# Low parts written over the raw weights, four buffers for the high parts, and the loads gated by TensorE

## What is computed

```python
proj = h @ w_in             # several, 2048 deep, up to 6680 wide; also w_out, w_kv, w_cq ...
x = x + y @ w_out
scores -> top 16 of 128x128 keys per head -> gate[token, expert]
a = gelu(h @ w_u.T) * gate  # w_u: 16384 x 2048
x = x + a @ w_v             # w_v: 16384 x 2048
```

## Time and profile before

| | us |
|---|---|
| median of 3 runs | 3142.95 |
| the profiled execution | 3144.03 |
| its span (first to last instruction) | 3141.9 |
| TensorE busy | 3003.1 |
| VectorE busy | 1890.5 |
| ScalarE busy | 1363.6 |

### The profile page before, as it was taken

How to read it: one execution, slowest core, us unless ns; L and a number is a source line. 1 busy time by engine, 2 the same in 40 slices (tenths; PEclk the granted TensorE clock), 3 DMA queues, 4 the chain that set the end, 5 groups by cost and what they waited for, 6 DMA issues and landing times. The chain is left out here.

```text
span 3141.9 us, 41649 instructions
## 1 busy us (share of the span) xinstructions
PE 3003.1 (96%) x16258; PEld 2576.6 (82%) x16258; DVE 1890.5 (60%) x2383; ACT 1363.6 (43%) x1511; POOL 5.3 (0%) x8
## 2 busy tenths in 40 slices
PE   8999978899998999999899999999999999999998
PEld 6878777789877788877899988878888888888887
DVE  4546775555676544565568988855555445554445
ACT  4543454444444343345434444433344344434344
POOL 0000000000000000000000000000000000000000
PEclk9999999899999999999999999999999999999999
DMA  6554435145442555444345455565655655545553
GB/s 249 187 189 175 175 129 175 59 163 188 161 169 103 178 184 183 165 155 161 129 156 184 164 186 206 203 234 187 241 187 187 241 196 188 189 175 194 207 191 143
DMA packets 94113, 560.54 MB, mean 178 GB/s; under 512 B 10552, under 2 KB 26544, under 8 KB 31920
## 3 DMA queue, kind: packets, MB, share of 16 engines
q1 hardware_dynamic: 73152, 522.03, 47.1%
q10 hardware_dynamic: 20848, 36.95, 3.1%
HBM read 543.15 MB, written 15.73 MB: 178 GB/s over the span
## 5 line engine op out<-in xcount | busy, mean ns | idle before, releaser
L2052 DVE TENSOR_TENSOR w_lo<-raw,w_hi 128x2048 fp32r<-128x2048 f32 (+2 forms) x500 | 1130.7, 2262 | 1100.7 <-ACT w_hi L1354 1095.8
L1354 ACT ACTIVATE w_hi<-raw 128x2048 fp32r<-128x2048 f32 (+2 forms) x500 | 945.6, 1892 | 1182.8 <-PE ps L767 414.5
L765 PE MATMUL ps<-w_hi,hT 128*128 128x512 f32 (+3 forms) x1344 | 523.6, 390 | 28.9 <-DVE w_lo L2052 28.4
L767 PE MATMUL ps<-w_hi,hT 128*128 128x512 f32 (+3 forms) x1344 | 515.4, 383 | 0.0
L766 PE MATMUL ps<-w_lo,hT 128*128 128x512 f32 (+3 forms) x1344 | 515.1, 383 | 0.0
L1226 PE MATMUL ps<-hT,w_hi 128*128 128x512 f32 x1536 | 486.4, 398 | 1.2 <-DVE x L2982 0.7
L1268 PE MATMUL ps<-w_hi,c_hi 128*128 128x512 f32 x1024 | 401.1, 392 | 11.9 <-DVE c_lo L2942 11.9
L1270 PE MATMUL ps<-w_hi,c_lo 128*128 128x512 f32 x1024 | 399.8, 390 | 0.0
L1269 PE MATMUL ps<-w_lo,c_hi 128*128 128x512 f32 x1024 | 399.8, 390 | 0.0
L1230 PEld LDWEIGHTS ps<-hT,w_lo 128*128 128x128 f32 x1536 | 289.2, 188 | 68.5
L765 PEld LDWEIGHTS ps<-w_hi,hT 128*128 128x128 f32 x1344 | 255.6, 190 | 80.3 <-DVE w_lo L2052 23.5
(11 more groups left out here) (274 smaller groups left out, 3324.6 us busy)
## 6 DMA issues: line engine op xcount, KB each, us to landing
raw<-in_w_u_t SPq DMA_DIRECT2D x128, 1024.0 KB, 4.8
raw<-in_w_v SPq DMA_DIRECT2D x128, 1024.0 KB, 5.2
raw<-in_w_in_2.0 SPq DMA_DIRECT2D x32, 1024.0 KB, 4.7
raw<-in_odd_w.0 SPq DMA_DIRECT2D x20, 1024.0 KB, 4.7
raw<-in_even_w.3608 SPq DMA_DIRECT2D x16, 1024.0 KB, 4.9
raw<-in_w_out.0 SPq DMA_DIRECT2D x16, 1024.0 KB, 4.8
raw<-in_w_out.1 SPq DMA_DIRECT2D x16, 1024.0 KB, 4.8
raw<-in_w_out_2.0 SPq DMA_DIRECT2D x16, 1024.0 KB, 4.8
```

What stands on the lines that cost most here:

```text
L765: pe.matmul(o, hi, wh, start=(j + k == 0), stop=False)
L767: mm = pe.matmul(o, lo, wh, start=False, stop=(j == 3 and k == 3))
L1354: act.activation(w_hi[:, s % 2, 0:size], raw[:, s, 0:size], ACT.Copy).then_inc(hi_done, 1)
L2052: dve.tensor_tensor(w_lo[:, s % 2, 0:size], raw[:, s, 0:size], w_hi[:, s % 2, 0:size].bitcast(F32), ALU.subtract).then_inc(lo_done, 1)
```

## The change

SBUF use stays the same: 64 KB of each partition held four raw buffers and two each for w_hi and w_lo, and now hold four for w_lo and four for w_hi. `raw` is a second name for the memory of `w_lo` (the same address, type float32). DVE now writes the low part of an item over its raw values. Four things follow in the code:

- The load of item n waits until PE has finished item n-4 (`item_used`), where it waited for DVE's split of item n-4.
- ACT's split waits for the landing alone. That the buffers are free follows from the landing, since the load waited for PE.
- PE, ACT and DVE take buffer n % 4 (in unrolled loops `s` or `j`) in place of n % 2.
- In six places (seven waits, since one stands in a program run for both layers) ACT's side work, which read what ACT itself had evacuated, now waits for its own evacuation (`evac_act`).

The order of instructions on every engine is as it was. What has changed is what they wait for; ACT's 24 register instructions that worked out the values of the removed wait in loops are gone too.

```diff
+RAW_AT = 4096 + 4 * (NT * D + KC * 2 * S)
...
-    raw = sb("raw", [P, RAW, 2048])
-    w_hi = sb("w_hi", [P, 2, 2048], F32R)
-    w_lo = sb("w_lo", [P, 2, 2048], F32R)
+    w_lo = sb("w_lo", [P, RAW, 2048], F32R)
+    w_hi = sb("w_hi", [P, RAW, 2048], F32R)
+    raw = nc.alloc_sbuf_tensor_at("raw", [P, RAW, 2048], F32, offset=RAW_AT)
...
             if n >= RAW:
-                sp.wait_ge(lo_done, n - RAW + 1)
+                sp.wait_ge(item_used, n - RAW + 1)
...
                 for s in range(RAW):
-                    sp.wait_ge(lo_done, 4 * i + (base + s - RAW + 1))
+                    sp.wait_ge(item_used, 4 * i + (base + s - RAW + 1))
...
-                            wh = w_hi[:, j % 2, k * width:(k + 1) * width]
-                            wl = w_lo[:, j % 2, k * width:(k + 1) * width]
+                            wh = w_hi[:, j, k * width:(k + 1) * width]
+                            wl = w_lo[:, j, k * width:(k + 1) * width]
...
         def split(q, s, size):
 
-            if not isinstance(q, int) or 4 * q + s >= 2:
-                act.wait_ge(item_used, 4 * q + (s - 1))
             act.wait_ge(landed[s], 16 * q + 16)
-            act.activation(w_hi[:, s % 2, 0:size], raw[:, s, 0:size], ACT.Copy).then_inc(hi_done, 1)
+            act.activation(w_hi[:, s, 0:size], raw[:, s, 0:size], ACT.Copy).then_inc(hi_done, 1)
...
         def memory_side(l):
             loaded()
+            act.wait_ge(evac_act, g_m[l].act0 + 2)
             act.wait_ge(evac_dve, g_m[l].dve0 + 2)
...
             dve.wait_ge(hi_done, 4 * q + (s + 1))
-            dve.tensor_tensor(w_lo[:, s % 2, 0:size], raw[:, s, 0:size], w_hi[:, s % 2, 0:size].bitcast(F32),
+            dve.tensor_tensor(w_lo[:, s, 0:size], raw[:, s, 0:size], w_hi[:, s, 0:size].bitcast(F32),
                               ALU.subtract).then_inc(lo_done, 1)
```

More of the change, by code:

```diff
@@ L821, in out_part @@
                         hi, lo = hT_hi[:, 4 * j + k, t * P:(t + 1) * P], hT_lo[:, 4 * j + k, t * P:(t + 1) * P]
-                        wh, wl = w_hi[:, n % 2, k * COLS:(k + 1) * COLS], w_lo[:, n % 2, k * COLS:(k + 1) * COLS]
+                        wh, wl = w_hi[:, n % RAW, k * COLS:(k + 1) * COLS], w_lo[:, n % RAW, k * COLS:(k + 1) * COLS]
                         pe.matmul(o, hi, wh, start=begins and k == 0, stop=False)
@@ L962, in cmp_gemm @@
                         hi, lo = c_hi[:, q % 2, l * 32:l * 32 + 32], c_lo[:, q % 2, l * 32:l * 32 + 32]
-                        wh = w_hi[:, n % 2, l * CMP_HID:(l + 1) * CMP_HID]
-                        wl = w_lo[:, n % 2, l * CMP_HID:(l + 1) * CMP_HID]
+                        wh = w_hi[:, n % RAW, l * CMP_HID:(l + 1) * CMP_HID]
+                        wl = w_lo[:, n % RAW, l * CMP_HID:(l + 1) * CMP_HID]
                         first, last = q + l == 0, q == 3 and l == 7
@@ L1152, in _ @@
                     hi, lo = hT_hi[:, k, t * P:(t + 1) * P], hT_lo[:, k, t * P:(t + 1) * P]
-                    wh, wl = w_hi[:, n % 2, k * 512:(k + 1) * 512], w_lo[:, n % 2, k * 512:(k + 1) * 512]
+                    wh, wl = w_hi[:, n % RAW, k * 512:(k + 1) * 512], w_lo[:, n % RAW, k * 512:(k + 1) * 512]
                     pe.matmul(o, hi, wh, start=(k == 0), stop=False)
@@ L1201, in _ @@
                         kc = 4 * j + k
-                        pe.matmul(o, w_hi[:, n % 2, a:a + P], hT_hi[:, kc], start=first, stop=False,
+                        pe.matmul(o, w_hi[:, n % RAW, a:a + P], hT_hi[:, kc], start=first, stop=False,
                                   skip_group_check=True)
-                        pe.matmul(o, w_hi[:, n % 2, a:a + P], hT_lo[:, kc], start=False, stop=False,
+                        pe.matmul(o, w_hi[:, n % RAW, a:a + P], hT_lo[:, kc], start=False, stop=False,
                                   skip_group_check=True)
-                        mm = pe.matmul(o, w_lo[:, n % 2, a:a + P], hT_hi[:, kc], start=False, stop=last,
+                        mm = pe.matmul(o, w_lo[:, n % RAW, a:a + P], hT_hi[:, kc], start=False, stop=last,
                                        skip_group_check=True)
@@ L1225, in activations @@
                     for k in (k0, k0 + 1):
-                        pe.matmul(ps[:, s % 2, :], w_hi[:, s % 2, k * P:(k + 1) * P],
+                        pe.matmul(ps[:, s % 2, :], w_hi[:, s, k * P:(k + 1) * P],
                                   hT[:, k].rearrange("p n t -> p (n t)"), start=(k == 0), stop=False,
@@ L1229, in activations @@
                     for k in (k0, k0 + 1):
-                        mm = pe.matmul(ps[:, s % 2, 0:S], w_lo[:, s % 2, k * P:(k + 1) * P], hT_hi[:, k], start=False,
+                        mm = pe.matmul(ps[:, s % 2, 0:S], w_lo[:, s, k * P:(k + 1) * P], hT_hi[:, k], start=False,
                                        stop=(k == KC - 1), skip_group_check=True)
@@ L1236, in activations @@
             for k in range(KC):
-                wh, wl = w_hi[:, s % 2, k * P:(k + 1) * P], w_lo[:, s % 2, k * P:(k + 1) * P]
+                wh, wl = w_hi[:, s, k * P:(k + 1) * P], w_lo[:, s, k * P:(k + 1) * P]
                 pe.matmul(o, wh, hT_hi[:, k], start=(k == 0), stop=False)
@@ L1266, in outputs @@
                 ch, cl = c_hi[:, s % 2, t * P:(t + 1) * P], c_lo[:, s % 2, t * P:(t + 1) * P]
-                wh, wl = w_hi[:, s % 2, n * 512:(n + 1) * 512], w_lo[:, s % 2, n * 512:(n + 1) * 512]
+                wh, wl = w_hi[:, s, n * 512:(n + 1) * 512], w_lo[:, s, n * 512:(n + 1) * 512]
                 pe.matmul(o, ch, wh, start=first and b in fresh, stop=False, skip_group_check=True)
@@ L1521, in keys_side @@
         def keys_side():
+            act.wait_ge(evac_act, g_memkv[1].act0 + 2)
             act.wait_ge(evac_dve, g_memkv[1].dve0 + 2)
@@ L1582, in first_side @@
             yield from st.pair_at(AT_K)
+            act.wait_ge(evac_act, g_akv.act0 + 3)
             act.wait_ge(evac_dve, g_akv.dve0 + 3)
@@ L1590, in first_side @@
             yield from st.until(AT_B_SQUARES)
+            act.wait_ge(evac_act, g_b.act0 + 2)
             act.wait_ge(evac_dve, g_b.dve0 + 2)
@@ L1664, in first_side @@
             yield from st.until(AT_GATES)
+            act.wait_ge(evac_act, g_gz.act0 + 3)
             act.wait_ge(evac_dve, g_gz.dve0 + 3)
@@ L1741, in index_side @@
             yield from st.until(AT_C_SILU)
+            act.wait_ge(evac_act, g_cz.act0 + 3)
             act.wait_ge(evac_dve, g_cz.dve0 + 3)
```

## The result

The changed kernel took **3103.75 us** (median of 4 runs, 3102.60 to 3105.16) against 3142.97 us (4 runs, 3141.54 to 3145.56): ratio 0.9877, 95% interval 0.9865 to 0.9889. It is faster by 39.2 us. I had forecast 20 us, and 3103.75 lies under the range's lower end of 3111. The profiled execution took 3103.42 us, its span is 3101.3 us.

A forecast was written before the change was run, and what follows sets the result against it. TensorE, busy 3003.1 of 3141.9 us, was taken as the bound, so only its waits or clock drops could be won: 22.5 us won less 2.0 lost, 20.5 off 3144.0, about 3123 us for the median; range 3111 to 3137.

The forecast's parts named there:

- the slack: Usual cycle in V: time between a split item being ready and TensorE needing it grows from 1.2 to 6.7 us.
- the four waits named: TensorE's waits of L765 for w_lo at 149, 192, 477 and 928 us would be gone in the changed profile.
- those between 380 and 445 us: TensorE's waits of 4.3 and 1.9 us for w_lo and 13.6 us would stand, ACT and DVE being the limit; gain 0.
- the other edits: Waits on `evac_act`, subtraction over its own input, and four buffers in place of two: taken as costing 0.
- ACT and DVE were not the limit: Rival, chance 0.17: the chain of ACT and DVE takes the waits over; about 3135 us.
- TensorE's waits did not move elsewhere: Rival, chance 0.10: waits were hidden or merely move to attention, turns or barriers; gain within 6 us, 3137 to 3149 us.
- the usual load of V: Rival, chance 0.05, slower: in U and V, landings above 11.9 us put loads on TensorE's path; 3172 us at 12.1 us.
- U0, 3.8 in six: Loop U0: six TensorE waits on w_lo, 3.8 us in all, of which 3.0 us would be won.
- That is what the 18 waits are.: TensorE's waits on w_lo after the start, 30.2 us, come from ACT or DVE side work exceeding 1.2 us of slack.
- 320 to 345 us: Three TensorE waits, 4.3 us: the first two (1.6) go, the third (2.7) follows the last evacuation; 2.5 us won.
- I take one such loss: In V, one weight load near a fetch of gates lands after 13.5 us and costs TensorE 2.0 us.
- all 30.2 us go: Range's lower end: all w_lo waits in question and four clock drops of 1.5 us go, 36 us, 3107; range ended at 3111.

The follow-up runs named there:

- the gate: ACT's split of item n waits until TensorE ends item n-2, which the change removed; put back in every split of the new kernel: 3160.76 us.
- the gate in U0 alone: New kernel with ACT's wait for TensorE's end of item n-2 put back in the 32 splits of loop U0: 3116.60 us.
- the gate put back at three places: New kernel with ACT's wait for the end of item n-2 put back for items 88 to 111, 146 to 153 and 223 to 230: 3112.19 us.
- the two runs with the gate everywhere: New kernel with ACT's wait for the end of item n-2 in every split: 3160.76 us; the same with second and third fetch in pieces: 3150.74 us.
- the version with a lead of one item: New kernel with ACT's split of item n waiting for TensorE's end of item n-3: 3107.78 us.

## Why the prediction was half right

The mechanism was right: the gate made the waits (restored, it brings them back), the slack grew by 5.0 us, to 6.0, the four waits named went away at their places, those between 380 and 445 us stood, the other edits cost nothing, and a load behind a fetch came late. The rivals fell: ACT and DVE were not the limit at the places named, TensorE's waits did not move elsewhere, and the usual load of V takes its 5.3 us. What failed is the price: the prediction took the listed idle time of TensorE's waits on w_lo for the whole cost of the gate, and its range was built on that. The sizes one by one:

- **"U0, 3.8 in six, DVE is nearly full with choosing. I take 3.0."** The gate's part was 8.5, shown by the gate in U0 alone and its companions; another 1.6 us of the 10.1 were a drop of the clock at item 277 that one execution had and the other not, which is luck. I took the listed idle time for the price. A stall costs what lies between the starts, and here 0.66 us for 0.41 listed; eight of 14 stalls were listed nowhere. That DVE was nearly full was no limit: with a lead it was never late.
- **"That is what the 18 waits are."** The list of waits on w_lo is not the list of what the gate costs. 11.7 us were won in stretches for which I had no term (items 83 to 130, 146 to 160, 161 to 245), and the gate put back at three places there cost 6.2 us of it again. One form can be read off the views: ahead of item 150 TensorE waited 2.1 us at the matmuls of L823 for a turned activation, put down to issue. After the change that wait is gone, and with the gate back at items 146 to 153 it returns (the last row of that experiment). The other form is that of U0.
- **320 to 345 us, "I take 2.5"** was 5.1 over items 32 to 60. I had given back the third wait as fixed behind the last evacuation; it shrank from 2.70 to 1.76 us. Another 1.6 us are a drop of the clock at item 53 that the new kernel's profiled run lacks. That is luck too, since the same kernel profiled again has it. Most of the rest is the first two waits.
- **"I take one such loss", 2.0 us** was 8.5 us in two. The formula held: landing + 0.4 - 11.9 gives 2.6 and 4.0 us for landings of 14.1 and 15.5 us, and TensorE's waits are 2.63 and 3.99. The landing was wrong. The row of before that I used (13.5 us) was of a load issued 4.5 us behind its fetch. In the new kernel load and fetch are issued within 0.3 us of each other, since the load now waits for TensorE. And behind the longer stall the clock drops, 1.5 us more. The Trainium skill's rule that I had weighed ("DMA: Bandwidth & Descriptors", Issuing engines are not separate DMA queues) gave each of the three fetches a late load; here the trace agrees for the second and the third, while beside the first, at 2019 us, no load took over 9 us. What came late there was the store ahead of it, at item 308 (1.5 us).

In sum: 34.8 us where the terms had 22.5, 11.7 us without a term, 0.1 us between, and 6.0 lost from item 331 on where I had 2.0, which makes the 40.6 us up to item 499. The lower end failed by the same step: "all 30.2 us go" was a bound on listed waits, not on the gate's cost.

## What to carry to other kernels

Price a stall of TensorE by the distance between the starts of its matmuls, or by the distance between the same item's ends, and not by the listed idle time; count the items that begin at the moment their input is ready, since they are the ones a lead will free. Before you credit a stretch to a change, look at whether its items show the same clock in several executions. When a change moves loads to a later release, look at what else is issued within a few tenths of a microsecond of them: here a load issued just behind a big transfer landed together with it. A large prefetch that nobody needs soon belongs in pieces.

## What the runs showed of the hardware

- A 1 MB load that was issued up to 0.3 us behind a 4 MB fetch from another engine landed after 14.1, 15.5 and 16.2 us, with the fetch, against 5.3 us alone; 0.16 us ahead of the fetch it took 10.2 us, 0.46 us ahead 5.1. Beside 0.5 MB pieces loads took 5.0 to 8.4 us. A 384 KB store took 2.7 us with the last load issued 5.2 us ahead of it, and 3.7 to 6.4 us in the eleven runs where a load was issued 2.5 us ahead. A 16 KB transfer took 6.2 us in the kernel before, 12.0 and 12.8 us in the two runs with the gate everywhere, and 7.9 to 10.6 us in the other nine.
- Whether the clock drops behind a stall is not a matter of the stall alone. At the second fetch TensorE waited 2.63 us in the new kernel and came back at the full clock, and 2.88 us in the version with a lead of one item and came back at half (1.2 GHz). At item 372 it waited 2.81 us in every one of the twelve profiled runs: in five the item took 5.7 us at the full clock, in seven 7.1 to 7.4 us with a drop. The 2 us from its start at the second fetch (window, engines' busy us, then the granted clock), first the new kernel's, then the other's:

```profile
2172.30:2174.30 2.00, 2.00 (x9) 1.66 (x10) 2.00 (x1) 1.63 (x2) 0.00 (x0) 1.00 0.98 397
```

```profile
2178.30:2180.30 2.00, 1.99 (x5) 1.60 (x6) 2.00 (x1) 1.40 (x2) 0.00 (x0) 0.50 0.92 385
```

  Such a drop mostly cost 1.5 to 1.7 us, in two cases of the run with U0 gated more (items of 8.6 us). How many fall in one execution differs; runs of one and the same kernel here spread by 2.6 to 9.3 us.
